# Every fourth v row summed by VectorE, five v row slots, one query pass for three tiles, mixing spread over the expert stage

## The reference, cut to what matters

```python
def block(args):                        # one block of 128 tokens
    tb, ib, gb = args                   # tokens, 128 expert numbers and weights per token
    a = jax.nn.gelu(jnp.einsum('tkd,td->tk', jnp.take(u_tab, ib, axis=0), tb))
    return jnp.einsum('tk,tkd->td', gb * a, jnp.take(v_tab, ib, axis=0))
```

## Time and profile before

| | |
|---|---|
| runs | 5133.36, 5126.46, 5130.38 us; median 5130.38 |
| the profiled execution | 5130.07 us, span 5128.2 us |
| TensorE, VectorE, GpSimd, ScalarE busy | 4041.2, 3196.4, 2499.6, 590.6 us |
| moved by DMA | 1596.30 MB, of them 1342.34 MB by the gathers' queue |
| prompt tiles (first to last dot product) | 394.1 to 916.4 us, 2896.1 to 3419.4 us |
| sample tiles, first layer | 1088.4 to 2774.9 us |
| sample tiles, second layer | 3590.0 to 5060.1 us |

### The profile page before, as it was taken

One profiled execution on the slowest core, in us unless ns is written; L12 is line 12 of the kernel. 1 busy time (PEld: TensorE's weight loads), 2 busy tenths in 40 slices (PEclk: granted clock), 3 DMA queues, 4 the chain that ended last, 5 costly groups with the idle time before them and its releaser, 6 DMA issues.

```text
span 5128.2 us, 36856 instructions
## 1 busy us (share of the span) xinstructions
PE 4041.2 (79%) x10767; PEld 1795.4 (35%) x10767; DVE 3196.4 (62%) x7509; ACT 590.6 (12%) x1232; POOL 2499.6 (49%) x2570
## 2 busy tenths in 40 slices
PE   8889788848778878877878977978487887677677
PEld 4554333323233333343343433433233333222223
DVE  1167887467666765555544779672776677766663
ACT  1130321010000000011000214101000000000000
POOL 0003455226666655544544244550566666656674
PEclk9898899979999999988989979989799999999999
DMA  8546789559999989988989377983899999889997
GB/s 266 179 137 246 231 286 330 183 189 406 406 355 371 396 338 378 391 311 299 386 330 339 130 255 233 330 314 112 314 406 356 379 392 359 334 347 376 359 408 292
DMA packets 557942, 1596.30 MB, mean 311 GB/s; under 512 B 51424, under 2 KB 176944, under 8 KB 556466
## 3 DMA queue, kind: packets, MB, share of 16 engines
q0 software_dynamic: 368640, 1342.34, 69.4%
q1 hardware_dynamic: 188530, 251.45, 14.3%
q10 hardware_dynamic: 576, 0.16, 0.0%
HBM read 1590.99 MB, written 2.79 MB: 311 GB/s over the span
## 4 chain that ended last, share of the span: by engine, by line
DMA 31%; PE 30%; DVE 17%; POOL 10%; issue 7%; DVEq 2%; SPq 1%; ACT 1%; PEldq 0%; PEld 0%; POOLq 0%; ACTq 0%
DMA rows<-in_peer_u_dram,idx 14%; DMA rows<-in_peer_v_dram,idx 14%; POOL rows L2164 10%; PE ps L1297 10%; PE ps L840 6%; DVE rows L2053 5%; PE ps L847 5%; DVE work L2095 3%; PE ps L810 2%; PE ps L880 1%; DMA ring<-in_w_ada_dram 1%; SPq L674 1%; DMA ring<-in_w_in_dram 1%; DVEq L1930 1%; DVE work L1921 1%
## 5 line engine op out<-in xcount | busy, mean ns | idle before, releaser
L1297 PE MATMUL ps<-rows,work 128*128 128x512 f32 x4096 | 1990.4, 621 | 474.5 <-DMA rows<-in_peer_v_dram,idx 431.9
L2053 DVE CUSTOM_DVE_ANT_0 rows<-rows,ps 128x1024 f32<-128x1024 f32 x1024 | 1247.4, 1219 | 1048.5 <-DMA rows<-in_peer_u_dram,idx 1036.3
L2164 POOL DMA_INDIRECT rows<-in_peer_v_dram,idx x1280 | 1249.5, 976 | 1303.8 <-PE ps L1297 682.1
L2164 POOL DMA_INDIRECT rows<-in_peer_u_dram,idx x1280 | 1249.3, 976 | 1298.9 <-DVE idx L2046 660.2
L1297 PEld LDWEIGHTS ps<-rows,work 128*128 128x128 f32 x4096 | 745.1, 196 | 1621.1 <-issue 1336.8
L840 PE MATMUL ps<-h_s,ring 128*128 128x512 f32 x1024 | 469.6, 615 | 52.2 <-DVE work L1841 48.3
L2053 DVE CUSTOM_DVE_ANT_0 rows<-rows,work 128x1024 f32<-128x1024 f32 x256 | 312.2, 1224 | 141.0 <-DMA rows<-in_peer_u_dram,idx 135.0
L2128 DVE TENSOR_SCALAR work<-cst,acts,g_w 128x128 f32<-128x128 f32 x1024 | 365.1, 359 | 41.7 <-PE ps L1297 18.9
L2095 DVE SCALAR_TENSOR_TENSOR work<-rows,acts,work 128x1024 f32<-128x1024 f32 x254 | 325.5, 1281 | 21.0 <-DMA rows<-in_peer_v_dram,idx 16.8
L840 PEld LDWEIGHTS ps<-h_s,ring 128*128 128x128 f32 x1024 | 200.3, 198 | 314.2 <-issue 309.5
L840 PE MATMUL ps<-work,ring 128*128 128x512 f32 (+1 forms) x768 | 263.0, 496 | 7.4 <-DVE work L1845 3.1
(11 more groups left out here) (289 smaller groups left out, 3062.6 us busy)
## 6 DMA issues: line engine op xcount, KB each, us to landing
ring<-in_w_in_dram SPq DMA_DIRECT2D x68, 1024.0 KB, 11.4
ring<-in_peer_wq_dram SPq DMA_DIRECT2D x64, 1024.0 KB, 11.0
ring<-in_w_ada_dram SPq DMA_DIRECT2D x48, 1024.0 KB, 13.9
rows<-in_peer_u_dram,idx POOLq DMA_INDIRECT x1280, 7.2
rows<-in_peer_v_dram,idx POOLq DMA_INDIRECT x1280, 7.0
ring<-in_w_out_dram SPq DMA_DIRECT2D x16, 1024.0 KB, 5.5
ring<-in_tables_dram SPq DMA_DIRECT2D x10, 1024.0 KB, 8.5
ring<-in_w_in_dram SPq DMA_DIRECT2D x8, 832.0 KB, 6.3
```

The source lines that it names most:

```text
L1297: mm = pe.matmul(y_acc[:, cols], diag[:, e % TOPK, :], rows[:, ROWS + s, cols], start=e == 0, stop=e == EXPERTS - 1)
L2053: dve.tensor_tensor_reduce(rows[:, s, :], rows[:, s, :], tok, 1.0, 0.0, ALU.mult, ALU.add, dots[:, e:e + 1]).then_inc(rows_u_free, 1)
L2164: pool.indirect_dma_start(rows[:, slot0 + s, :], None, table, bass.IndirectOffsetOnAxis(ap=idx[:, t % 2, e:e + 1], axis=0)).then_inc(came[ ...
```

## The change

It does five things.

1. Of a sample tile's v rows, those with e divisible by `EACH` = 4 are no longer multiplied by TensorE. VectorE adds them, `Y_LAG` = 27 slots behind its dots, into a buffer `y_d`; at the tile's end TensorE adds `y_d` into `y_acc` with an identity matmul of two halves. The weights (gelu times gate) are now multiplied once for 16 rows (`w_s`), and the diagonal takes one scalar.
2. The sample tiles have five v buffers (`ROWS_V`), the fifth in the work area. Two semaphores count free v rows, one for those that VectorE adds and one for TensorE's; a gather waits for the one of the row that was last in its buffer. `V_SLOT` holds buffer, arrival count and that former row.
3. Tiles 1, 2 and 3 share one query pass (before: tile 1 alone, then 2 and 3), so `peer_wq` is read twice a layer for the sample instead of three times.
4. The mixing stages are laid over other slots: queries 17 to 156 (before 20 to 130 and 135 to 290), condition vectors 157 to 252 (292 to 364), prompt mixing 253 to 472 (365 to 480), its queries 473 to 508 (481 to 508); in the second layer the final norms from slot 160, with five slots from step to step instead of three. `SPREAD` is 0.97 instead of 0.9. The selection parts from group 4 on start 46 slots ahead of their use instead of 64.
5. For the prompt ScalarE's gate activation stands at the second half of its matmuls in the order, not at the first.

The diff, without the places that only follow from it (the buffers' views, the prompt tile's same waits under new names):

```diff
 ROWS = 4
+ROWS_V = 5
+EACH = 4
+Y_LAG = 27
...
 QUERIES_P = [Inst("Q", l) for l in range(LAYERS)]
-QUERIES_S = [[Inst("Q", l, True, tiles) for tiles in ((0,), (1,), (2, 3))] for l in range(LAYERS)]
+QUERIES_S = [[Inst("Q", l, True, tiles) for tiles in ((0,), (1, 2, 3))] for l in range(LAYERS)]
...
 SAMPLE_SLOTS = STILES * EXPERTS + 40
-SPREAD = 0.9
+SPREAD = 0.97
...
-    first, step = {0: (FIRST_SLOT, 1), 1: (1, 2), 2: (12, 5), 3: (38, 5)}.get(group, (PER_GROUP * group - 64, 6))
+    first, step = {0: (FIRST_SLOT, 1), 1: (1, 2), 2: (12, 5), 3: (38, 5)}.get(group, (PER_GROUP * group - 46, 6))
...
-        over(q1, 20, 130)
-        over(q2, 135, 290)
+        over(q1, 17, 156)
...
             ada, pr, qp = ADAS[l + 1], PROMPTS[l + 1], QUERIES_P[l + 1]
-            over(ada, 292, 364)
-            over(pr, 365, 480)
-            over(qp, 481, 508)
+            over(ada, 157, 252)
+            over(pr, 253, 472)
+            over(qp, 473, 508)
...
             for n, i in enumerate(LASTS):
-                at = 292 if i.l == STILES else max(304 + 12 * n, (i.l + 1) * EXPERTS + M_LAG + 12)
-                steps += [(at + 3 * k, PLACE[i, name]) for k, (name, _) in enumerate(turn_order(i))]
+                at = 160 if i.l == STILES else max(184, (i.l + 1) * EXPERTS + M_LAG + 12)
+                steps += [(at + 5 * k, PLACE[i, name]) for k, (name, _) in enumerate(turn_order(i))]
...
+def v_slots():
+    table, came, last = {}, [0] * ROWS_V, [None] * ROWS_V
+    for t in range(LAYERS * TILES):
+        for e in range(EXPERTS):
+            s = ((t % TILES - 1) * EXPERTS + e) % ROWS_V if t % TILES else e % ROWS
+            came[s] += 1
+            table[t, e] = (s, came[s], last[s])
+            last[s] = t * EXPERTS + e
+    return table
+V_SLOT = v_slots()
+def by_vector(t, e):
+    return t % TILES == 0 or e % EACH == 0
+def v_ends():
+    table, done = {}, {False: 0, True: 0}
+    for t in range(LAYERS * TILES):
+        for e in range(EXPERTS):
+            done[by_vector(t, e)] += 1
+            table[t, e] = done[by_vector(t, e)]
+    return table
+V_END = v_ends()
+def added_by_tensor(t, e):
+    rows = [V_END[a, b] for a in range(t + 1) for b in range(EXPERTS) if (a, b) <= (t, e) and not by_vector(a, b)]
+    return max(rows, default=0)
...
                         j, e = at_n // EXPERTS, at_n % EXPERTS
-                        t, s = tile_of(l, True, j), e % ROWS
-                        pe.wait_ge(diag_ready, (first + j) * EXPERTS + e + 1)
-                        pe.wait_ge(rows_v_in[s], 16 * ((t * EXPERTS + e) // ROWS + 1))
+                        t = tile_of(l, True, j)
+                        s, came, _ = V_SLOT[t, e]
+                    if at_n >= 0 and not by_vector(t, e):
+                        pe.wait_ge(diag_ready, V_END[t, e])
+                        pe.wait_ge(rows_v_in[s], 16 * came)
...
                             cols = slice(half * 512, (half + 1) * 512)
-                            mm = pe.matmul(y_acc[:, cols], diag[:, e % TOPK, :], rows[:, ROWS + s, cols],
-                                           start=e == 0, stop=e == EXPERTS - 1)
-                        mm.then_inc(rows_v_free, 1)
+                            mm = pe.matmul(y_acc[:, cols], diag[:, e % TOPK, :], v_row_of(t, e)[:, cols],
+                                           start=e == 1, stop=False)
+                        mm.then_inc(rows_v_free[False], 1)
                         if e == EXPERTS - 1:
+                            pe.wait_ge(yd_ready, first + j + 1)
+                            for half in range(2):
+                                cols = slice(half * 512, (half + 1) * 512)
+                                mm = pe.matmul(y_acc[:, cols], ident, y_d[:, cols], start=False, stop=True)
+                            mm.then_inc(yd_used, 1)
...
                 for r, (b, t) in enumerate(slots):
-                    yield PLACE[i, ("gate", b, t)]
+                    yield PLACE[i, ("gate" if i.sample else "gateb", b, t)]
...
                     dve.drain()
-                    if t >= 2:
-                        dve.wait_ge(rows_v_free, (t - 1) * EXPERTS)
+                    if added_by_tensor(t - 2, EXPERTS - 1):
+                        dve.wait_ge(rows_v_free[False], added_by_tensor(t - 2, EXPERTS - 1))
...
                     w = n - W_LAG
-                    if w >= 0:
+                    if 0 <= w < STILES * EXPERTS:
...
                             head_weights(t, e // TOPK)
-                        row = first * EXPERTS + w
+                            hs = slice(e, e + TOPK)
+                            dve.tensor_tensor(w_s[:, hs], acts[:, hs], g_w[:, t % 2, hs], ALU.mult)
+                            dve.drain()
...
                             before = w - TOPK
-                            dve.wait_ge(rows_v_free, tile_of(l, True) * EXPERTS + before + 1)
-                        dve.tensor_scalar(diag[:, e % TOPK, :], ident, acts[:, e:e + 1], g_w[:, t % 2, e:e + 1],
-                                          ALU.mult, ALU.mult).then_inc(diag_ready, 1)
+                            dve.wait_ge(rows_v_free[False], added_by_tensor(tile_of(l, True, before // EXPERTS),
+                                                                            before % EXPERTS))
+                        if not by_vector(t, e):
+                            dve.tensor_scalar(diag[:, e % TOPK, :], ident, w_s[:, e:e + 1], None, ALU.mult)\
+                                .then_inc(diag_ready, 1)
+                    w = n - Y_LAG
+                    if w >= 0 and by_vector(tile_of(l, True, w // EXPERTS), w % EXPERTS):
+                        add_row(l, w // EXPERTS, w % EXPERTS)
...
+            def add_row(l, j, e):
+                t = tile_of(l, True, j)
+                s, came, _ = V_SLOT[t, e]
+                dve.wait_ge(rows_v_in[s], 16 * came)
+                if e == 0:
+                    if l or j:
+                        dve.wait_ge(yd_used, l * STILES + j)
+                    ins = dve.tensor_scalar(y_d, v_row_of(t, e), w_s[:, e:e + 1], None, ALU.mult)
+                else:
+                    ins = dve.scalar_tensor_tensor(y_d, v_row_of(t, e), w_s[:, e:e + 1], y_d, ALU.mult, ALU.add)
+                ins.then_inc(rows_v_free[True], 1)
+                dve.drain()
+                if e == EXPERTS - EACH:
+                    dve.sem_inc(yd_ready, 1)
...
-            def gather(t, e, table, slot0, free, came):
+            def gather(to, t, e, table, came):
+                pool.indirect_dma_start(to, None, table, bass.IndirectOffsetOnAxis(
+                    ap=idx[:, t % 2, e:e + 1], axis=0)).then_inc(came, 16)
+            def u_row(t, e):
                 s, row = e % ROWS, t * EXPERTS + e
-                if row >= ROWS:
-                    pool.wait_ge(free, row + 1 - ROWS)
-                pool.indirect_dma_start(rows[:, slot0 + s, :], None, table, bass.IndirectOffsetOnAxis(
-                    ap=idx[:, t % 2, e:e + 1], axis=0)).then_inc(came[s], 16)
-            def u_row(t, e):
...
                     pool.wait_ge(idx_ready, GROUPS * t + e // PER_GROUP + 1)
-                gather(t, e, u_rows, 0, rows_u_free, rows_u_in)
+                if row >= ROWS:
+                    pool.wait_ge(rows_u_free, row + 1 - ROWS)
+                gather(rows[:, s, :], t, e, u_rows, rows_u_in[s])
             def v_row(t, e):
+                s, _, before = V_SLOT[t, e]
...
                     pool.wait_ge(idx_ready, GROUPS * (t + 1))
-                gather(t, e, v_rows, ROWS, rows_v_free, rows_v_in)
+                if t % TILES == 1 and ROWS <= e < ROWS_V:
+                    pool.wait_ge(x_done, t)
+                if before is not None:
+                    was = before // EXPERTS, before % EXPERTS
+                    pool.wait_ge(rows_v_free[by_vector(*was)], V_END[was])
+                gather(v_row_of(t, e), t, e, v_rows, rows_v_in[s])
```

More of the change, by code:

```diff
@@ L355, in cuts @@
     for l in range(LAYERS):
-        s, (q0, q1, q2) = SAMPLES[l], QUERIES_S[l]
+        s, (q0, q1) = SAMPLES[l], QUERIES_S[l]
         for place, share in mix_share(s):
@@ L483, in build @@
         acts = sb("acts", [P, EXPERTS])
+        w_s = sb("w_s", [P, EXPERTS])
         top_p = sb("top_p", [P, 1, 2 * 2 * PH * TOPK])
-        WORK = 17664
+        WORK = 17792
         work = sb("work", [P, WORK])
@@ L560, in scratch, with v_row_of @@
             return v
+        y_d = view(16768, D)
+        def v_row_of(t, e):
+            s = V_SLOT[t, e][0]
+            return rows[:, ROWS + s, :] if s < ROWS else view(15744 + (s - ROWS) * D, D)
         scratch_p = scratch(rows_flat[:, ROWS * D:ROWS * D + SCRATCH])
@@ L630, in build @@
         rows_u_in = [sem(f"rows_u_in{s}") for s in range(ROWS)]
-        rows_v_in = [sem(f"rows_v_in{s}") for s in range(ROWS)]
-        rows_u_free, rows_v_free = sem("rows_u_free"), sem("rows_v_free")
+        rows_v_in = [sem(f"rows_v_in{s}") for s in range(ROWS_V)]
+        rows_u_free = sem("rows_u_free")
```

(14 more changed lines are left out.)

## The result

The changed kernel takes 5479.82 us (median of four runs, 5471.2 to 5496.02) against 5128.91 us: a ratio of 1.0687, 95% interval 1.0657 to 1.0716. Forecast were 5302 us in a range of 5050 to 5420. The direction and the mechanism held, the size was half of what came: +342.6 us of span where the sum said +172.

The account below looks back on a forecast made before the run. Transfers set the smooth pace, 2.56 us a slot, raised by GpSimd's stalls on TensorE; the change adds a stop every fourth slot. Second layer +171, first +37, less 16 for tails and 20 for density: +172, 5302 us, range 5050 to 5420.

Parts of the forecast that it names:

- The rule that decides: At every fourth v gather GpSimd must stop until VectorE finishes slot w+27; its lead falls from four dots to two.
- the round: Four sample-tile slots from one add's end to the next: 6.7 + L, 12.9 us, 3.22 a slot against 2.84 before.
- L: Time from start to landing of the fourth gather after a stop; taken as 6.2 us, 0.1 us being worth 25 us.
- such lumps: VectorE's selection and key-search work falling before a stop in sample tiles: 20 us for the first layer, nothing for the second.
- the ring: Cycle in the sample tiles: add frees a gather, later gathers follow, the fourth lands, its dot runs, then the next add.
- Tails: Last 22 v rows at a layer's end: five slots for four shorten TensorE's rows, 8 us saved a layer.
- Density: Prompt tiles, 0.9 to 0.97: sample mixing moves into the prompt tile, worth 0 to 34 us a layer, 10 taken.
- TensorE's stalls: GpSimd's waits on TensorE in sample tiles, 431 and 210 us by layer, would go; nothing else counted for them.
- The stretches of tiles 3 and 4: First layer: 3.51 us a slot under condition loads, 3.33 under the prompt's weights; both tiles get shorter.
- Rival 3: Sample tiles: L stays 7.0 or more, or VectorE's lumps land on the stop; round 13.7, 5501 us, chance 0.06.
- Rivals 1, 2 and 4: Sample tiles with L of 5.2 (5074 us, chance 0.16), 4.3 (4891, 0.11) or near 5.4 (5130, 0.03).
- rival 2: Sample tiles: the stop costs nothing, L is a lone gather's 4.3, round 11.0; 4891 us, chance 0.11.

## Why the prediction came out as it did

**The rule that decides** was right, in place and in kind. GpSimd stops 230 times on the add, nearly every fourth v gather; the add two slots earlier or no stop at all take the loss away, the stop without the add brings most of it, and a sixth buffer takes nearly all of that away again.

**What was mis-sized: the round.** The sum had 0.27 + 3.73 + L + 2.7. The same parts as means over the 121 rounds of each layer, worked out from the starts and landings in the trace:

| part of the round, us | forecast | first layer | second layer |
|---|---|---|---|
| add's end to the freed gather | 0.27 | 0.38 | 0.38 |
| to the fourth gather | 3.73 | 3.90 | 3.79 |
| its landing, L | 6.2; 6.7 as a mean in layer 1 | 6.81 | 6.20 |
| landed to its dot's start | nothing | 0.42 | 0.44 |
| dot's start to the add's end | 2.7 | 2.69 | 2.69 |
| round | 12.9; 13.4 in layer 1 | 14.2 | 13.5 |

L, on which all the rivals turned, came out to the hundredth as a mean of the second layer. That close a hit is luck, since it was taken from a single gather of 6.3 us; single rounds start from 5.1 us. What failed is the step that lets the dot start when its row lands, a term that the sum put at nothing. 0.13 us pass even in the median round, and 0.3 more on average: in 58 of the 242 rounds the dot starts over 0.2 us late, and in 57 of these VectorE was still at work when the row landed, with a piece of the selection, a key search, a norm, some other mixing work or the dot before. The prediction costed such lumps ("nothing for the second") and put at most 15 us a tile on them. They are 15 us in each layer's first tile and fall to 3 or 4 in its last, 35 and 38 us a layer. With 0.06 to 0.17 for slower issues, 0.11 at the release and, in the first layer, 0.1 of L, a round is 0.8 us longer than forecast in the first layer and 0.6 in the second, 97 and 74 us over 121 rounds. In the first layer the sum had 20 of them for lumps, and 70 of the rest show; in the second 70 show. The ends of the layers, where no stop comes any more, run a little ahead of the sum.

So the lesson of the size is: the ring has no slack, and every small thing on it counts 242 times. The sum took the clean instance of each part for its mean. That 0.1 us of round is 25 us stood in the rivals, but only L was varied by it.

**Tails, forecast -16 us, came out at +10.** The fifth buffer was to shorten TensorE's last rows. But the add's lag holds for the last rows too: the stop at the layer's end lets its gather go at 5405.56, 3 us behind the last dot's start, and the identity passes come behind it. At the end of the first layer the gap grew by 9.6 us. What each of the two, stop and identity pass, makes of it was not tried. The part was worked out as if all rows were still TensorE's.

**Density, forecast -20 us, measured -18.2.** The prompt tiles are 19.4 and 14.0 us longer by their dots, the gaps behind them 26.9 and 24.6 shorter. ScalarE's later gate wait falls in the same stage and was not told apart.

**TensorE's stalls** went as forecast, by 560 us of 641; and as forecast nothing of it reaches the end.

**The stretches of tiles 3 and 4** were forecast as shorter, and are, though as part of a first layer that is longer. They are 3.56 us a slot by their dots, against 3.33 to 3.51 in the sum; the landing under the condition loads, 7.31 us, was taken well (7.35), under the prompt's weights it is 6.86 for 6.6, and there the issues take 4.04 for 3.73; the rest is the table's.

**The rivals.** Rival 3 gave its time, 5501, to an L of 7 "or lumps on VectorE land on the stop". The run lies near its number, but not for its reason in the second layer: L is 6.2, and from each layer's second tile on no piece lies on the stop until it is put there (5592); in the first tile one does, 3.5 us a layer. Rivals 1, 2 and 4 needed an L under 5.5; no tile's mean is under 6.1. With rival 2 falls the rule of the Trainium skill that was weighed ("DMA: Bandwidth & Descriptors", on the anatomy of one DMA). The four gathers of the burst at 5208.90 land after 4.3, 6.0, 5.7 and 6.3 us. By the page's constant and bytes, plus the issue, the estimate was some 4.1: the first agrees with it, and the others, issued behind it, don't.

**What the profile was to show:** waits on the add some 250 times at 3 us: 230 at 3.8. Round near 12.9: 13.2 at the median of the second layer's last three tiles, 13.5 as the layer's mean. Landings about 6: 6.2 and 6.4. Last tile at about 325 GB/s: 318. Each of these was near; only their sum over 242 rounds was not.

## What to carry to other kernels

Follow each release of a buffer around: the requests that it lets go, up to the one that the next release depends on, then that one's landing and its readers. This chain has to be shorter than the time that the transfers of as many slots take (here 10.2 us for four). Where it is longer, a single late reader in four turns a full queue into a ring of latencies, and each slot more costs in full. Where an in-order engine issues the requests hardly faster than they are served, a stop wasn't made good later. Where work is moved from one engine to another to relieve stalls, try the cheaper cures first: here one or two more buffers and an even layout gave 141 to 175 us, with all rows left where they were.

## What the runs showed of the hardware

TensorE's clock fell though it had less to do: granted 0.80 in the last tile with 61% of it busy, 0.97 with 74% before and 0.99 with 77% in the version with six buffers. That is a mix of its two levels, 2.4 and 1.2 GHz, and the v matmuls took 742 ns in the mean instead of 621. TensorE waited for rows anyhow (797 us before the largest group of v matmuls), so little can hang on it here; whether the idle time lowered the clock was not tried by itself. A thinned queue didn't shorten the landing of a burst's fourth gather: 6.3 us at 318 GB/s in the change, 6.3 at the start of a burst in the earlier trace rows; the first takes 4.3 in both.
